# Mixer A of a two-mixer transformer block: the low part of a pair's queries four projection blocks later

## Chip, cores and metric

One core of a Trainium2 chip (trn2) runs the kernel as one program. The metric is the device time of one execution in microseconds (us). PE is TensorE, DVE VectorE, ACT ScalarE, POOL GpSimd and SP SyncE, which issues the DMAs.

## The reference, cut to what matters

The input runs through two blocks of layers. The first block has a mixer A (grouped attention with a rotary encoding over rows and columns) and a mixer B (neighbourhood attention), each on 512 tokens of `x` and 256 tokens of context. The change lies in mixer A:

```python
def gqa_axial_mixer(hx, hc, w_in, q_g, k_g, w_out, cos, sin, need_ctx_out):
    px = hx @ w_in
    q = px[..., :A_WIDTH].reshape(b, t, A_HEADS, HEAD_DIM)        # 16 heads of 64
    ...
    z = px[..., A_WIDTH + 2 * A_KV_WIDTH:]                        # the gate
    q = apply_axial_rope(rms_norm(q, q_g), cos, sin)
    ...
        s = jnp.einsum('bqkgd,bskd->bkgqs', qi, k_all).astype(jnp.float32) * ATTN_SCALE
        p = jax.nn.softmax(s, axis=-1).astype(v_all.dtype)
        return jnp.einsum('bkgqs,bskd->bqkgd', p, v_all)
    ...
    yx = (o * jax.nn.silu(z)) @ w_out
    ...
    qc = rms_norm((hc @ w_in[:, :A_WIDTH]).reshape(b, lc, A_HEADS, HEAD_DIM), q_g)
    zc = hc @ w_in[:, A_WIDTH + 2 * A_KV_WIDTH:]
    sc = jnp.einsum('bqkgd,bskd->bkgqs', qc, kc).astype(jnp.float32) * ATTN_SCALE
```

Everything is float32. A matrix product is made of three on PE: each operand is split into a high part (a rounded copy) and a low part (what the rounding left), and high x high, high x low and low x high are summed.

## The kernel before, in words

**Order of the work.** `build` first writes a list, `plan`, of named items with `do(...)` (L331). Then each engine walks the whole list and issues its own instructions for the items that it has a part in (`program`, L1441). So an engine's queue has the order of the list, and semaphores join the engines. PSUM banks are handed out by rings (`Ring.take`, L160), and the first matmul into a bank waits for the bank's last reader.

**Mixer A.** The 16 heads are worked on in 8 pairs. A pair has six score steps (tiles of 128 queries): four tiles of `x`, with 768 keys (weight 1.0 for the planner), and two of the context, with 256 keys (weight 0.7). So steps 6p to 6p+5 belong to pair p, 48 in all. In a step (`scores` L678, `trans` L698, `outp` L708): PE makes the scores of both heads into all four banks of one ring (L1551), DVE takes maxima (L2170, L2179), ACT exponentials (L1830), DVE reciprocals (L2186), POOL multiplies (L2560), PE transposes the probabilities (L1561) of the step before, ACT and DVE copy them out (L1840, L2195), and PE makes the outputs (L1586) of two steps before, which DVE multiplies with the gate (L2206, for the last pair L2208).

**The fill.** Between these, PE works on projections, drawn block by block from the generator `fill_a` (L861). For pair 1 to 7 it holds four groups of 8 blocks: the queries of `x` and of the context (`query_group`), and the gate of `x` (`gate_group(pair, 0, ...)`) and of the context (`gate_group(pair, 1, ...)`). A block is one of eight slices of the inner dimension, three matmuls, over 512 columns for `x` (5.12 units) or 256 for the context (2.56 units) (`pj` L411; PE L1463 to L1465). `fill_in` (L715) gives each half of a step its share of the units that are left, and stops early at a negative value (`PAUSE`). The dictionary `between` names what is emitted after a block: `between.get(k)` is called when the generator is resumed after block k, ahead of block k+1. After the fill of pair 7 comes `begin_out` (L828), the first blocks of the output projection: per block of `k` a part 0 to 6 (`parts`: ACT cast L1792, then a subtraction on POOL, L2534, for even `k`, on DVE, L2090, for odd), then two blocks of 5.12.

**The query's chain.** While a pair's gate is projected, its queries are finished: sums and turn on PE (L1528, L1534), rotation on DVE and POOL (L2134, L2553, L2140), `a_query_high` (ACT cast, L1812), `a_query_low` (DVE subtraction, L2144: `qL = qT - qH`). The scores read `qH` and `qL`. `query_low(pair)` (L782) plans `a_query_low` and adds the pair to `ready_q`. Tile 0 of a pair isn't planned before (L809 to L811), and `attention` (L665) draws more blocks until it is:

```python
while not todo[n][0]():
    x = more()
```

`a_gate` (ACT L1820, DVE L2150) ends each gate group. In pair 7 the context's gate group carries a modulation unit as well: `ride_mm_x` after block 3 (16 matmuls, L1476, into bank 6) and `ride_tr` after block 6 (L1484).

Of the kernel before, what the change touches and what calls it, by code (L numbers as in the profile page):

```python
# [166 lines left out]
def build(nc, wu, vp, cc, cs1, xt, biasb, pos, out):  # L167
    ctx = ExitStack()
    with ctx:
# [92 lines left out]
        def bank(b, n=512):  # L262
            return PS[:, 512 * b:512 * b + n]
# [67 lines left out]
        def do(*item):  # L331
            plan.append(item)
            done_work[0] += COST.get(item[0], 0)
# [9 lines left out]
        def ring(*groups):  # L343
            return Ring(Order, *groups)
# [66 lines left out]
        def pj(key, un, lo, hi, f0, phase, o, ks=range(8)):  # L411

            groups[key] = Group(key, un.n, False, lo, hi, f0, 128, phase, o)
            for k in ks:
                if k % 4 == 3:
                    tick()
                do("proj", key, k)
                yield (hi - lo) / 100
# [238 lines left out]
        def until(cond):  # L657
            while not cond():
                yield BLOCK
# [89 lines left out]
        OA, FA, FX, FC = ring((5,)), ring((6,), (7,)), ring((6,)), ring((7,))  # L749
# [7 lines left out]
        def query_group(pair, j, pr, between={}):  # L757

            if j == 0:
                aun[pair] = Unit("aqz", pair)  # L760
            lo, hi = FULL[j]
            o = bank(pr.take(("aq", pair, j), (s_qraw, (pair, j))))
            for k in range(8):
                yield from pj(("aq", pair, j), aun[pair], lo, hi, 0, "a", o, (k,))
                between.get(k, nothing)()
            do("a_query_raw", pair, j)

        def query_sums(pair, pr):
            aqps[pair, "sums"] = bank(pr.take(("aqs", pair), (s_qvar, (pair,))))
            do("a_query_sums", pair)  # L770

        def query_turn(pair, pr):
            aqps[pair, "rot"] = bank(pr.take(("aqr", pair), (s_qsin, (pair,))))
            do("a_query_turn", pair)

        def query_rope(pair):
            do("a_query_rope", pair)

        def query_high(pair):
            do("a_query_high", pair)  # L780

        def query_low(pair):  # L782
            do("a_query_low", pair)
            ready_q.add(pair)

        def gate_group(pair, j, pr, between={}):
            lo, hi = FULL[j]
            o = bank(pr.take(("az", pair, j), (s_gate, ("a", pair, j))))
            for k in range(8):
                yield from pj(("az", pair, j), aun[pair], lo, hi, 128, "a", o, (k,))  # L790
                between.get(k, nothing)()
            do("a_gate", pair, j)
            if j:
                ready_z.add(pair)
                aun[pair].done(s_proj, "az", pair, 1)
# [32 lines left out]
        def begin_out(name, phase, part, done, pr):  # L828


            un = Unit(name, 0)
            led = {(m, 0): bank(pr.take((name, m, 0), (s_res, (name, m, 0)))) for m in (0, 1)}
            for k in range(10):
                if k < 7:
                    yield from until(lambda: k in done)
                    part(k)
                    yield 3 if k not in (1, 2) else PAUSE
                if k >= 3:
                    for m in (0, 1):
                        yield from pj((name, m, 0), un, 0, T, 128 * m, phase, led[m, 0], (k - 3,))  # L840
            begun[name] = un, led
# [19 lines left out]
        def fill_a():  # L861
            for pair in range(1, 8):
                yield from query_group(pair, 0, FX, {2: ride_mm, 6: ride_tr})
                yield PAUSE
                yield from query_group(pair, 1, FC)
                yield PAUSE
                yield from until(lambda: pair < 2 or 6 * pair - 7 in scored_a)
                yield from gate_group(pair, 0, FX, {2: lambda: query_sums(pair, FC), 3: lambda: query_turn(pair, FC), 5: lambda: query_rope(pair), 7: lambda: query_high(pair)})
                yield PAUSE
                yield from gate_group(pair, 1, FC, {1: lambda: query_low(pair), **({3: ride_mm_x, 6: ride_tr} if pair == 7 else {})})  # L870
                yield PAUSE
            yield from begin_out("aout", "o", parts_a, done_a, FA)
        values((0, 1))
# [15 lines left out]
        query_high(0)  # L889
        run(gate_group(0, 1, vr, {3: lambda: query_low(0)}))  # L890
        attention("a", [s for pair in range(8) for s in steps_a(pair)], SA, TA, PbA, PTbA, OA, fill_a(), (8 * 14 * (T + LC) + 14 * T) / 100 + 5 * 3, posted_a, scored_a.add)
        do("a_last_gate")

# [459 lines left out]
        OC, FC = ring((4,)), ring((5,), (6,), (7,))  # L1353
# [1495 lines left out]
```

## Time and profile before

| | before |
|---|---|
| median of 3 runs | 1624.19 us (1623.81 to 1627.51) |
| the profiled execution | 1623.98 us |
| its span | 1622.2 us |
| mean granted TensorE clock | 0.978 |
| PE busy | 1534.7 us (95%) |
| DVE busy | 754.4 us (47%) |
| ACT busy | 640.9 us (40%) |
| POOL busy | 688.1 us (42%) |

Times of a row are counted from the start of the span. Mixer A's score steps run from 110 to about 458 us. Matmuls overlap: the duration of a group is from the start of its first to the modelled end of its last, and the next one may start before that. A granted clock of 1.00 is 2.4 GHz, 0.50 is 1.2 GHz.

### The profile page before, as it was taken

The numbers are of one execution on the slowest core, as the hardware profiler recorded it, in microseconds if no ns is written. First come the engines' busy times: TensorE is split into PE (matmuls) and PEld (weight loads), VectorE is DVE, ScalarE is ACT, GpSimd is POOL, SyncE is SP. The second block draws the span as 40 slices with busy tenths as digits, with TensorE's granted clock in tenths as the row PEclk, the third lists the DMA queues.
The fourth block names the chain that finished last, engine by engine and source line by source line (L and its number), as shares of the span: only waits on it lengthen the run. The fifth ranks groups of instructions, "written<-read, shape, count | busy, mean of one in ns | idle before, by whom it ended". The sixth has DMA issues, their size and how long they took to land.

```text
span 1622.2 us, 25653 instructions
## 1 busy us (share of the span) xinstructions
PE 1534.7 (95%) x10114; PEld 1244.3 (77%) x10114; DVE 754.4 (47%) x1733; ACT 640.9 (40%) x1339; POOL 688.1 (42%) x660
## 2 busy tenths in 40 slices
PE   5999999999899999999998899999999989999997
PEld 3887777777688788787876687878787867766875
DVE  4444555555532534534355454733432564455253
ACT  4234444444532533433334353434332344443331
POOL 2534444443432533433325444535255434444462
PEclk8999999999999999999999999999999999999998
DMA  9111111110233222322321222222131221111221
GB/s 396 44 67 38 42 53 53 53 53 28 72 100 128 78 72 82 108 79 79 105 92 43 100 85 78 79 68 88 52 104 53 92 91 53 53 53 53 94 88 52
DMA packets 22438, 129.80 MB, mean 80 GB/s; under 512 B 2480, under 2 KB 2608, under 8 KB 8368
## 3 DMA queue, kind: packets, MB, share of 16 engines
q1 hardware_dynamic: 22176, 127.92, 22.8%
q8 instruction: 80, 1.31, 0.3%
q10 hardware_dynamic: 144, 0.26, 0.1%
q14 instruction: 38, 0.31, 0.1%
HBM read 126.08 MB, written 2.10 MB: 79 GB/s over the span
## 4 chain that ended last, share of the span: by engine, by line
PE 80%; DVE 9%; ACT 3%; POOL 3%; issue 3%; DMA 1%; SPq 0%; POOLq 0%; DVEq 0%; ACTq 0%
PE PS L1463 15%; PE PS L1465 15%; PE PS L1464 15%; PE PS L1586 6%; PE PS L1561 6%; PE PS L1544 4%; PE PS L1458 3%; PE PS L1459 3%; PE PS L1460 3%; PE PS L1551 3%; DVE sm L2170 2%; PE PS L1639 1%; PE PS L1631 1%; PE PS L1476 1%; DMA XC<-in_xt 1%
## 5 line engine op out<-in xcount | busy, mean ns | idle before, releaser
L2493 POOL TENSOR_TENSOR WL<-W,WH 128x512 fp32r<-128x512 f32 x304 | 400.4, 1332 | 330.9 <-ACT WH L1742 330.6
L1463 PE MATMUL PS<-HX,WH 128*128 128x512 f32 x1008 | 420.3, 417 | 11.8 <-DVE LX L2083 3.9
L1465 PE MATMUL PS<-HX,WL 128*128 128x512 f32 x1008 | 399.1, 396 | 0.0
L1464 PE MATMUL PS<-LX,WH 128*128 128x512 f32 x1008 | 398.2, 395 | 0.0
L1463 PEld LDWEIGHTS PS<-HX,WH 128*128 128x128 f32 x1008 | 193.1, 192 | 62.0 <-issue 17.1
L1465 PEld LDWEIGHTS PS<-HX,WL 128*128 128x128 f32 x1008 | 192.0, 190 | 42.6
L1464 PEld LDWEIGHTS PS<-LX,WH 128*128 128x128 f32 x1008 | 192.7, 191 | 35.8 <-issue 2.6
L1742 ACT CAST WH<-W 128x512 fp32r<-128x512 f32 x320 | 186.8, 618 | 42.0 <-PE PS L1460 25.6
L1830 ACT ACTIVATE AR<-PS,sm 128x768 f32<-128x768 f32 (+4 forms) x160 | 115.7, 723 | 165.2 <-DVE sm L2175 93.7
L2170 DVE TENSOR_REDUCE sm<-PS 128x1 f32<-128x512 f32 (+4 forms) x224 | 149.9, 669 | 43.7 <-PE PS L1551 39.3
L2560 POOL TENSOR_SCALAR AR<-AR,sm 128x768 f32<-128x768 f32 (+1 forms) x96 | 77.1, 804 | 186.2 <-DVE sm L2186 186.0
L2560 POOL TENSOR_SCALAR XC<-XC,sm 128x512 f32<-128x512 f32 x64 | 45.1, 704 | 163.2 <-DVE sm L2186 163.2
L1561 PE MATMUL PS<-C,AR 128*128 128x128 f32 x608 | 101.9, 285 | 10.0 <-DVE AR L2206 9.9
L1840 ACT COPY AR<-PS 128x512 f32<-128x512 f32 (+1 forms) x112 | 62.2, 556 | 109.4 <-PE PS L1561 108.4
L1586 PE MATMUL PS<-AR 128*64 128x128 f32 x1408 | 96.7, 282 | 5.8 <-DVE AR L2195 4.1
L1830 ACT ACTIVATE XC<-PS,sm 128x512 f32<-128x512 f32 x64 | 44.2, 690 | 145.2 <-DVE sm L2175 145.2
L1561 PEld LDWEIGHTS PS<-C,AR 128*128 128x128 f32 x608 | 69.3, 142 | 35.8 <-DVE AR L2206 12.8
L1458 PE MATMUL PS<-WH,HX 128*128 128x256 f32 x320 | 95.0, 297 | 0.8 <-POOL WL L2493 0.8
L1463 PE MATMUL PS<-HC,WH 128*128 128x256 f32 (+1 forms) x304 | 95.1, 313 | 0.5 <-POOL LC L2517 0.5
L1586 PEld LDWEIGHTS PS<-AR 128*64 128x64 f32 x1408 | 77.1, 139 | 23.9 <-issue 11.6
L1459 PE MATMUL PS<-WH,LX 128*128 128x256 f32 x320 | 91.2, 285 | 0.0
L1460 PE MATMUL PS<-WL,HX 128*128 128x256 f32 x320 | 91.2, 285 | 0.0
(290 smaller groups left out, 2546.3 us busy)
## 6 DMA issues: line engine op xcount, KB each, us to landing
W<-in_wu SPq DMA_DIRECT2D x98, 1024.0 KB, 4.9
AR<-in_wu SPq DMA_DIRECT2D x8, 1024.0 KB, 11.1
AR<-in_biasb SPq DMA_DIRECT2D x32, 256.0 KB, 2.7
XX<-in_xt SPq DMA_DIRECT2D x2, 1024.0 KB, 6.2
out<-XX SPq DMA_DIRECT2D x8, 256.0 KB, 2.2
XX<-in_xt SPq DMA_DIRECT2D x2, 768.0 KB, 5.3
XC<-in_xt SPq DMA_DIRECT2D x1, 1024.0 KB, 14.2
C<-in_cc SPq DMA_DIRECT2D x1, 770.5 KB, 8.7
```

The lines of the kernel that those rows point to most:

```text
L1458: e.matmul(o, xh, wh, start=(k == 0), stop=False)
L1459: e.matmul(o, xl, wh, start=False, stop=False)
L1460: t = e.matmul(o, xh, wl, start=False, stop=(k == 7))
L1463: e.matmul(o, wh, xh, start=(k == 0), stop=False)
L1464: e.matmul(o, wh, xl, start=False, stop=False)
L1465: t = e.matmul(o, wl, xh, start=False, stop=(k == 7))
L1561: t = e.transpose(o[:, j * 128:j * 128 + 128], s.pb[h][:, (q0 + j) * 128:(q0 + j) * 128 + 128], c("id"))
L1586: t = e.matmul(s.out[h], s.values[h][j], s.pt[h][:, j * 128:j * 128 + 128], start=(j == 0 and s.first), stop=(j == nv - 1 and s.final))
L1742: e.copy(WH[:, PART[n], a:z], W[:, n % 2, a:z]).then_inc(*s_wh.by(n, q))
L1830: e.activation(s.pb[h][:, 0:s.n], PS[:, s.score[h]:s.score[h] + s.n], ACT.Exp, bias=smn[:, i % 4:i % 4 + 1], scale=(1.0 if s.scale is None ...
L2170: e.tensor_reduce(mx, x, AX.X, ALU.max).then_inc(*s_max.by(name, n, h))
L2493: e.tensor_tensor(WL[:, d, a:z], W[:, n % 2, a:z], WH[:, d, a:z].bitcast(F32), ALU.subtract).then_inc(*s_wl_pool.by(n, q))
```

## The change

In the context's gate group `query_low(pair)` is called after block 5 and not after block 1, for pairs 1 to 7. Pair 0 has a call of its own, which stays. Nothing else is edited; the planner derives the rest of the list from it.

```diff
@@ -867,7 +867,7 @@
                 yield from until(lambda: pair < 2 or 6 * pair - 7 in scored_a)
                 yield from gate_group(pair, 0, FX, {2: lambda: query_sums(pair, FC), 3: lambda: query_turn(pair, FC), 5: lambda: query_rope(pair), 7: lambda: query_high(pair)})
                 yield PAUSE
-                yield from gate_group(pair, 1, FC, {1: lambda: query_low(pair), **({3: ride_mm_x, 6: ride_tr} if pair == 7 else {})})
+                yield from gate_group(pair, 1, FC, {5: lambda: query_low(pair), **({3: ride_mm_x, 6: ride_tr} if pair == 7 else {})})
                 yield PAUSE
             yield from begin_out("aout", "o", parts_a, done_a, FA)
```

## Rows read from the trace of the kernel before

**Rows 1.** The page: PE's busy time, and the chain that ended last.
```profile
PE 1534.7 (95%) x10114; PEld 1244.3 (77%) x10114; DVE 754.4 (47%) x1733; ACT 640.9 (40%) x1339; POOL 688.1 (42%) x660
...
PE 80%; DVE 9%; ACT 3%; POOL 3%; issue 3%; DMA 1%; SPq 0%; POOLq 0%; DVEq 0%; ACTq 0%
```

**Rows 2.** Waits of PE, 100 to 470 us: us in total, times, longest.
```profile
PE PS L1551 <- ACT AR L1830: 3.0, 3, 1.9
PE PS L1551 <- DVE XX_parts L2144: 2.1, 1, 2.1
```

**Rows 3.** The source line L2144: duration ns min/median/max, first and last start us.
```profile
L2144 DVE TENSOR_TENSOR XX_parts<-AR,XX_parts x8: 939/940/1202, 108.2 to 412.7; 128x768 fp32r<-128x768 f32 x8
```

**Rows 4.** Timeline, pair 2, steps 11 and 12: start us, us, engine line [idle before].
```profile
154.11 0.15 DVE L2186 RECIPROCAL sm<-sm 128x1 f32<-128x1 f32 x1
...
155.38 1.32 PE L1551 MATMUL PS<-AR_parts,XX_parts 64*128 64x512 f32 x12
```

**Rows 5.** Timeline, pair 5: the last reciprocal of step 29, and score 30.
```profile
328.82 0.16 DVE L2186 RECIPROCAL sm<-sm 128x1 f32<-128x1 f32 x1 [0.66 <-ACT AR L1830]
328.99 1.33 PE L1551 MATMUL PS<-AR_parts,XX_parts 64*128 64x512 f32 x12
```

**Rows 6.** Timeline, pair 6: last reciprocal of step 35, scores 36 and 37.
```profile
369.42 0.16 DVE L2186 RECIPROCAL sm<-sm 128x1 f32<-128x1 f32 x1
...
369.82 1.32 PE L1551 MATMUL PS<-AR_parts,XX_parts 64*128 64x512 f32 x12
...
375.29 1.32 PE L1551 MATMUL PS<-AR_parts,XX_parts 64*128 64x512 f32 x12 [0.82 <-ACT AR L1830]
```

**Rows 7.** Timeline, pair 7: context blocks 1 and 2, gate product, a_query_low, score 42.
```profile
410.75 0.28 PE L1463 MATMUL PS<-HC,WH 128*128 128x256 f32 x1
...
411.11 0.28 PE L1463 MATMUL PS<-HC,WH 128*128 128x256 f32 x1
...
412.05 0.69 DVE L2150 SCALAR_TENSOR_TENSOR AR<-AR,PS 128x512 f32<-128x512 f32 x1 [1.40 <-ACT AR L1820]
412.65 0.95 DVE L2144 TENSOR_TENSOR XX_parts<-AR,XX_parts 128x768 fp32r<-128x768 f32 x1
...
413.75 1.32 PE L1551 MATMUL PS<-AR_parts,XX_parts 64*128 64x512 f32 x12 [2.12 <-DVE XX_parts L2144]
```

**Rows 8.** Timeline, step 42 after its score: modulation, second exponential's end, score 43, its maximum.
```profile
416.31 1.07 PE L1476 MATMUL PS<-W,sm 128*32 128x256 f32 x16
...
418.86 0.18 ACT L1830 ACTIVATION_READ_ACCUMULATOR AR<-PS,sm 128x1 f32 x1
...
420.36 1.33 PE L1551 MATMUL PS<-AR_parts,XX_parts 64*128 64x512 f32 x12
...
421.71 0.96 DVE L2170 TENSOR_REDUCE sm<-PS 128x1 f32<-128x768 f32 x1 [0.41 <-PE PS L1551]
```

**Rows 9.** Timeline: score 44, subtractions of part 1, outputs in steps 44 and 45.
```profile
426.45 1.73 PE L1551 MATMUL PS<-AR_parts,XX_parts 64*128 64x512 f32 x12 [1.88 <-ACT AR L1830]
...
427.68 1.05 DVE L2090 TENSOR_TENSOR LX<-AR,HX 128x512 fp32r<-128x512 f32 x1 [2.42 <-ACT HX L1792]
...
428.65 0.94 DVE L2090 TENSOR_TENSOR LC<-AR,HC 128x256 fp32r<-128x256 f32 x1
...
429.98 2.83 PE L1586 MATMUL PS<-AR 128*64 128x128 f32 x24 [1.80 <-DVE AR L2195]
...
438.85 1.53 PE L1586 MATMUL PS<-AR 128*64 128x128 f32 x24
```

**Rows 10.** Stretches of 2 us: busy us of engines, PEclk (granted clock), DMA share, GB/s.
```profile
427.00:429.00 2.00, 1.18 (x10) 0.82 (x6) 1.32 (x2) 2.00 (x6) 2.00 (x2) 0.54 0.00 0
429.00:431.00 2.00, 1.02 (x10) 1.02 (x12) 1.97 (x5) 0.26 (x1) 1.22 (x3) 0.50 0.03 8
431.00:433.00 2.00, 2.00 (x19) 1.67 (x16) 0.25 (x2) 0.00 (x0) 1.93 (x3) 0.50 0.00 0
433.00:435.00 2.00, 2.00 (x11) 1.82 (x11) 0.92 (x3) 1.10 (x2) 0.00 (x0) 0.76 0.00 0
```

## The prediction

> **What bounds the kernel now.** I read the page first. TensorE (PE) is busy for 95% of the span and holds 80% of the chain of work that ended last [rows 1]: an engine other than PE costs time only where PE stands and waits for it. Then I asked who waited for whom on PE in mixer A (100 to 470 us). The operation that the change moves, a_query_low on VectorE (DVE, L2144), ends a PE wait once in the whole kernel, for 2.1 us; the exponentials on ScalarE (ACT, L1830) end three waits of 3.0 us in total [rows 2]. The eight a_query_low take 0.94 us each, one of them 1.20 [rows 3]. So the change works on what is behind 0.94 us of DVE work, and it can only matter where PE has little in hand.
>
> For the places I need the order of the program. Its planner writes one list, and every engine runs its own part of it in that order. A score step n takes all four banks of the score ring, so its matmuls wait for both exponentials of step n-1; the first step of a pair (6 x pair) also waits for that pair's a_query_low, and it isn't planned before `ready_q` holds the pair. I worked through the planner from the units that it spends: a context block costs 2.56, an x block 5.12, and a step's half draws blocks until its share is spent. What follows "four blocks later" differs by pair. Note that a function between two blocks is emitted when the generator is resumed, that is ahead of the next block.
>
> **Pairs 1 to 4: same blocks, later DVE slot, 0 us.** Block 5 is the last one drawn in the first score step of the group, so a_query_low slips into the following step, behind that step's first reciprocal and ahead of the gate product, still before the first score step of the pair. For pair 2 that reciprocal starts at 154.11 and takes 0.15, so the operation would run from about 154.2 to 155.1; score 12 starts at 155.38 [rows 4]. It stays hidden by some 0.2 us, by the two context blocks and the chain of exponentials. The old slot cost PE nothing either, so nothing is won. Bounds: 0 (hidden) and 0.1 us each if it takes its longest duration [rows 3]; I take 0.
>
> **Pair 5: +0.95 us.** Here the group began half a step later, and the operation lands behind the second reciprocal of step 29, one step-half before score 30. That reciprocal starts at 328.82 and takes 0.16; score 30 starts at 328.99, right behind PE's last block [rows 5]. After the change DVE does 0.94 us between the two: 329.9, and with the 0.05 of a semaphore score 30 starts at about 329.95. Nothing covers it, since the remaining blocks are before it already. Below: 0, if the reciprocal comes earlier because a_query_low no longer stands ahead of step 29's maxima; but the second of these waits in DVE's order behind the output of step 27, which that does not move.
>
> **Pair 6: +0.65 us.** Block 5 is the last one drawn before score 36, so the planner has to draw block 6 as well to emit a_query_low. PE does the same work (0.36 us for a context block, from one block's start to the next one's [rows 7]), but score 36 is now behind it and behind DVE: the reciprocal at 369.42, then 0.94, so 370.45 where it was 369.82 [rows 6]. And this delay is not absorbed: score 37 stood waiting for ACT for 0.82 us [rows 6], so the chain from score 36 sets its time, and the block moved ahead is no cover there. Bounds 0.35 (the block alone) and 0.9 (the operation at its longest).
>
> In one row more (the 1.20 us instance) a_query_low ran beside a probability product of GpSimd (POOL) that had just started, the other seven had 0.94 to 0.97. The Trainium skill, GPSIMD Engine Reference, section 1, says that GpSimd's SBUF interfaces are shared with VectorE and contend with DVE instructions that have two SBUF inputs, which this one has; by it 0.26 us would come on top in pairs 5 and 6, so +2.1 in place of +1.6.
>
> **Pair 7: -1.4 us.** Here the real change of order is. The step before it is through with the x group when score 42 is due, and the planner is forced on until a_query_low is out. Before: context blocks 0 to 2, then score 42, which stood idle for 2.12 us until a_query_low had ended at 413.60 [rows 7]. After: blocks 0 to 6, with the modulation unit that rides after block 3 (16 matmuls, 1.0 us [rows 8]), then score 42. DVE's order doesn't change (gate product of the x group, then a_query_low), as the blocks put nothing on DVE. PE reaches the modulation unit at 412.0; it needs bank 6, which that gate product frees at 412.75 (412.05 + 0.69 [rows 7]). So 412.8 + 1.0 + three blocks of 0.36 = 414.9 for score 42, 1.15 us later than before. From a score step's start to the end of its second exponential was 5.29 us (413.75 to 418.86 + 0.18), and score 43 came at 420.36, because the modulation's small matmuls and block 7 stood ahead of it [rows 8]. These are out of the way now: score 43 at 414.9 + 5.3 + 0.1 = 420.3, unchanged. The idle 2.12 us has become some 0.8 ahead of score 42 and some 2.2 ahead of score 43.
>
> Then the planner's parts of the output projection (ACT cast, then a DVE or POOL subtraction) come a step earlier: parts 0 and 1 in step 42 rather than 43. The two DVE subtractions of part 1 (1.05 and 0.94 us [rows 9]) then stand ahead of the maximum of score 43 and wait for the casts, which end about 422.6: I get the maximum at 424.1 rather than 421.71 [rows 8]. Score 44 moves from 426.45 [rows 9] to some 428.4, with two blocks of the output projection (0.7 us each, an estimate from twice the context block) already done before it. Part 3 does the same to the maximum of score 44, once more about 2.2 us; but there the kernel before had its own stall of that size, for parts 1 and 2 stood at that place (429.98, PE idle 1.80 [rows 9]). So I find score 45 at its old time, 437.5, with two more blocks done, and steps 46 and 47, which PE bounds, are 2 x 0.7 = 1.4 us shorter. Bounds of the whole term: -3.3 (with the clock, below) and +2.4 (one of the two delays of a maximum, 424.1 less 421.7, is not absorbed and eats the gain).
>
> **The DMAs.** SP's queue is moved in one thing: the weight load that waits for the riding modulation unit goes out with it, 3.5 us sooner, and the reload of x behind it as well. Neither is waited for here. No instruction is added or taken out.
>
> **The clock.** PE is granted 2.4 GHz (1.00) up to 427 us, and then 0.54, 0.50, 0.50 and 0.76 over four stretches of 2 us, so half (1.2 GHz) until 434 [rows 10], behind a stretch with its idle waits ahead of scores 42 to 44. By rows it costs 2.83 - 1.53 = 1.3 us on one step's output matmuls [rows 9], and I add half of that for the six transposes behind them, which ran in it too: 1.9, an estimate. I assume that it falls once after the change as well, as the idle sum of this stretch is nearly the same. The Trainium skill, TensorE: Matmul & The Clock Gate, in its Terms, prices throttled time at that time x (1 - K/N), so 6.9 us x 0.5 = 3.4 us here; by it the fall that stays away would be worth -3.4, not -1.9. It says (Part 1) that recent activity is what releases the throttle: that speaks against the change where it takes cover away from behind score 42.
>
> **Sum.** 0 + 0.95 + 0.65 - 1.4 = +0.2 us. The profiled execution took 1623.98 us (a span of 1622.2 and 1.8 around it), so 1624.2 by its own time. The median of the runs is 1624.19, 0.2 above it, so 1624.4. About 0.3% (4.9 us) is what a measurement of this kernel can tell from no change.
>
> **The rivals.**
> B: the operation stays hidden everywhere and the planner's shift in pair 7 evens out; 1624.2. For it: PE's wait on a_query_low is 2.1 of 1622 us. Against it: rows 5 and 6 leave no room. Chance 0.15.
> C: the clock does not fall in step 44, since its idle time is spread differently, and pair 7 gives 1.4 + 1.9: 1624.4 - 1.9 = 1622.5, and 1620.9 if pairs 5 and 6 cost nothing too. For it: two blocks now lie ahead of score 44, where PE stood. Against: idle time after block 7 is new. Chance 0.20.
> D, slower: the subtractions of parts 1 and 3 in DVE's queue ahead of the maxima of scores 43 and 44 both reach the end, because the cover went before score 42. Each is 2.4 us, the 1.4 is gone: 1.6 + 4.8 = +6.4, so 1630.6. It decides if score 45 comes more than some 3 us later than 437.6. Against: PE had idle time there of the same size already. Chance 0.10.
> My forecast, near zero by cancelling terms: 0.55.
>
> The forecast's own range goes from -3.3 (1620.9) to 1.6 + 0.5 + 2.4 = +4.5 (1628.7); it takes in B and C, and leaves out D and the tails. Over 4.9 us faster needs nearly all idle time of steps 42 to 44 to vanish: 0.03. Slower by as much is most of D: 0.09. The same: 0.88.
>
> **What would show it.** Pairs 1 to 4: distances between the first scores of the pairs unchanged. Score 30 behind a_query_low with some 0.9 us of PE wait that is new, score 36 likewise with less. The 2.1 us wait ahead of score 42 gone or under 1 us, a new wait for ACT of 2 us ahead of score 43, and score 43 at 422 (420.4 and the 1.6 of pairs 5 and 6). The end of step 47 within 2 us of the old one. I am wrong if the pairs 1 to 4 shift, if the blocks are drawn elsewhere than I worked out, if the clock falls at another place or twice, or if anything behind 460 us changes its length.

## The result, and the profile after

| | before | after |
|---|---|---|
| median, runs side by side on one chip | 1624.72 us (10 runs, 1622.61 to 1627.51) | 1629.93 us (10 runs, 1627.55 to 1633.42) |
| the profiled execution | 1623.98 us | 1627.55 us |
| its span | 1622.2 us | 1625.6 us |
| mean granted TensorE clock | 0.978 | 0.977 |

The changed kernel is slower: the ratio is 1.0029, 95% interval 1.0019 to 1.0038, about 4.7 us. The forecast was +0.2 us with a range that ended at 1628.7. The median of 1629.93 lies 1.2 us beyond that. The difference is clear of the noise, though still inside the 0.3% that the prediction took as its bound.

The page of the kernel after, first two parts of it that answer to [rows 1]:

```profile
PE 1536.0 (94%) x10114; PEld 1245.5 (77%) x10114; DVE 755.9 (47%) x1733; ACT 640.8 (39%) x1339; POOL 689.1 (42%) x660
...
PE 78%; DVE 9%; ACT 4%; POOL 3%; issue 3%; DMA 1%; SPq 0%; POOLq 0%; DVEq 0%; ACTq 0%
```

No instruction was added (the same counts), and PE's share of the chain fell from 80 to 78%: the loss is waiting. The waits of PE, 100 to 470 us (us in total, times, longest), which answer to [rows 2]:

```profile
PE PS L1561 <- DVE AR L2206: 11.3, 13, 2.8
PE PS L1551 <- ACT AR L1830: 3.3, 3, 2.2
PE PS L1586 <- ACT AR L1840: 2.8, 3, 1.2
...
PE PS L1551 <- DVE XX_parts L2144: 1.1, 2, 0.9
PE PS L1561 <- DVE AR L2208: 1.1, 2, 0.8
PE PS L1476 <- DVE AR L2150: 0.8, 1, 0.8
```

The 2.1 us wait on a_query_low is gone. Two smaller ones on it have come (0.9 and 0.2), and one of 0.8 ahead of the modulation unit. Two groups of waits have grown or come that the prediction doesn't name: the outputs (L1586) for ACT's copies (2.8 us, before 0.9) and the transposes (L1561) for L2208 (1.1 us, before none).

**Pairs 5 and 6.** Timeline after, answering to [rows 5, 6] (start us, us, engine line):

```profile
326.84 0.16 DVE L2186 RECIPROCAL sm<-sm 128x1 f32<-128x1 f32 x1 [0.65 <-ACT AR L1830]
326.92 0.94 DVE L2144 TENSOR_TENSOR XX_parts<-AR,XX_parts 128x768 fp32r<-128x768 f32 x1
327.10 1.10 POOL L2560 TENSOR_SCALAR AR<-AR,sm 128x256 f32<-128x256 f32 x1 [0.34 <-DVE sm L2186]
...
328.00 1.32 PE L1551 MATMUL PS<-AR_parts,XX_parts 64*128 64x512 f32 x12 [0.93 <-DVE XX_parts L2144]
...
368.39 0.94 DVE L2144 TENSOR_TENSOR XX_parts<-AR,XX_parts 128x768 fp32r<-128x768 f32 x1
...
369.48 1.32 PE L1551 MATMUL PS<-AR_parts,XX_parts 64*128 64x512 f32 x12 [0.21 <-DVE XX_parts L2144]
```

The two profiled executions can be laid on each other instruction by instruction. Up to score 30 the one after is 1.98 us ahead; 1.6 of that comes from a half-clock stretch that only before has, at 147 us, and is no work of the change. Behind score 30 it is 0.99 ahead, behind score 36 0.34: so +0.99 and +0.65. In both places a_query_low took 0.94 us although POOL worked beside it; what got longer was POOL's product (1.10 us at 327.10, where the one of the same size just before took 0.48).

**Pair 7.** Timeline after, steps 42 to 44, answering to [rows 7, 8, 9]:

```profile
411.64 0.69 DVE L2150 SCALAR_TENSOR_TENSOR AR<-AR,PS 128x512 f32<-128x512 f32 x1 [1.40 <-ACT AR L1820]
...
412.38 1.07 PE L1476 MATMUL PS<-W,sm 128*32 128x256 f32 x16 [0.80 <-DVE AR L2150]
...
414.64 1.32 PE L1551 MATMUL PS<-AR_parts,XX_parts 64*128 64x512 f32 x12
...
420.11 2.04 PE L1551 MATMUL PS<-AR_parts,XX_parts 64*128 64x512 f32 x12 [2.17 <-ACT AR L1830]
...
421.88 1.67 DVE L2090 TENSOR_TENSOR LX<-AR,HX 128x512 fp32r<-128x512 f32 x1 [1.11 <-ACT HX L1792]
...
424.35 0.94 DVE L2170 TENSOR_REDUCE sm<-PS 128x1 f32<-128x768 f32 x1
...
429.53 1.82 PE L1551 MATMUL PS<-AR_parts,XX_parts 64*128 64x512 f32 x12
```

Start of each score step, and how long each lasts (from its start to the next one's; the last to the first block of the context's output projection, 458.66 and 459.39):

| step | 42 | 43 | 44 | 45 | 46 | 47 |
|---|---|---|---|---|---|---|
| starts, before | 413.75 | 420.36 | 426.45 | 437.56 | 444.60 | 451.60 |
| starts, after | 414.64 | 420.11 | 429.53 | 437.56 | 445.50 | 452.36 |
| lasts, before | 6.61 | 6.09 | 11.11 | 7.04 | 7.00 | 7.06 |
| lasts, after | 5.47 | 9.42 | 8.03 | 7.94 | 6.86 | 7.03 |

The execution after enters pair 7 with 0.41 ahead (its gate product at 411.64, before at 412.05) and leaves it 0.73 behind: +1.14 us where -1.4 was forecast. Score 42 comes 1.30 late by that measure; steps 42 to 44 then take 22.92 us where they took 23.81, so 0.41 of delay is left at score 45; step 45 adds 0.90; steps 46 and 47 give back 0.17 and not 1.4. What happens in steps 45 to 47, first before, then after:

```profile
437.43 0.69 DVE L2090 TENSOR_TENSOR LX<-AR,HX 128x512 fp32r<-128x512 f32 x1 [1.59 <-ACT HX L1792]
...
438.91 0.96 DVE L2170 TENSOR_REDUCE sm<-PS 128x1 f32<-128x768 f32 x1
...
444.62 0.58 ACT L1840 COPY AR<-PS 128x512 f32<-128x512 f32 x1
...
445.86 1.53 PE L1586 MATMUL PS<-AR 128*64 128x128 f32 x24 [0.64 <-DVE AR L2195]
445.92 1.14 ACT L1742 CAST WH<-W 128x512 fp32r<-128x512 f32 x2
...
456.12 0.66 PE L1586 MATMUL PS<-AR 128*64 128x128 f32 x8 [0.46 <-ACT AR L1840]
```

```profile
438.73 1.26 DVE L2090 TENSOR_TENSOR LX<-AR,HX 128x512 fp32r<-128x512 f32 x1 [1.66 <-ACT HX L1792]
...
440.25 0.94 DVE L2170 TENSOR_REDUCE sm<-PS 128x1 f32<-128x768 f32 x1
...
441.69 0.44 PE L1561 MATMUL PS<-C,AR 128*128 128x128 f32 x2 [0.77 <-DVE AR L2208]
...
445.54 1.14 ACT L1742 CAST WH<-W 128x512 fp32r<-128x512 f32 x2
...
446.58 0.58 ACT L1840 COPY AR<-PS 128x512 f32<-128x512 f32 x1
...
447.30 1.53 PE L1586 MATMUL PS<-AR 128*64 128x128 f32 x24 [1.18 <-ACT AR L1840]
...
456.86 0.66 PE L1586 MATMUL PS<-AR 128*64 128x128 f32 x8 [1.13 <-ACT AR L1840]
```

In step 45 the subtraction of part 5 stands ahead of the maximum, at 440.25 instead of 438.91; L2208 is behind that maximum in DVE's queue, and PE waits 0.77 for it. In steps 46 and 47 PE has one block less each (0.79 us from start to start), and its waits ahead of the outputs grow from 0.64 to 1.18 and from 0.46 to 1.13. The two steps lose their gain in different ways.

- Step 46: the wait stands ahead of the missing block, so the block's absence can't have made it. From the outputs to score 47 the step is 0.68 us shorter (451.60 - 445.86 before, 452.36 - 447.30 after). From score 46 to the outputs it is 0.54 longer (1.26 before, 1.80 after), because ACT now has the two weight casts (L1742, drawn together with the blocks) ahead of the copy that the outputs wait for: that copy starts at 446.58, where before it started at 444.62 and the casts came behind it at 445.92.
- Step 47: the missing block lay between its score and the wait at 456.86, and that distance is the same as before (4.50 and 4.52 us). It is set by the chain of maximum, exponential and ACT's copy, so here the saved work has become waiting.

**Mixer A in sum:** 0.99 + 0.65 - 0.07 (won back between score 36 and pair 7) + 1.14 = +2.7 us. The comparison says 4.7, so 2 us are left for what lies behind mixer A; in these two profiled executions it is 2.6. Where no granted clock differs the two executions keep their distance to some 0.03 us for hundreds of microseconds; it jumps only where one has half-clock time that the other hasn't. Stretches (PE, PEld, DVE, ACT, POOL busy us, then granted clock, DMA share, GB/s) of before, then of after:

```profile
840.00:1000.00 160.00, 144.08 (x775) 115.20 (x775) 86.88 (x149) 72.55 (x135) 76.97 (x68) 0.95 0.25 83
1000.00:1200.00 200.00, 200.00 (x1041) 167.04 (x1040) 85.80 (x136) 76.03 (x134) 85.95 (x73) 0.97 0.22 72
1200.00:1500.00 300.00, 291.12 (x1750) 219.55 (x1749) 147.14 (x418) 117.06 (x284) 139.53 (x145) 1.00 0.20 67
```

```profile
840.00:1000.00 160.00, 144.85 (x779) 116.52 (x776) 86.78 (x148) 71.95 (x134) 76.85 (x68) 0.93 0.24 82
1000.00:1200.00 200.00, 200.00 (x1045) 166.65 (x1044) 86.59 (x137) 76.53 (x135) 85.37 (x73) 0.98 0.22 74
1200.00:1500.00 300.00, 291.23 (x1743) 219.68 (x1743) 147.10 (x418) 117.04 (x284) 139.83 (x146) 0.99 0.20 67
```

After loses 1.9 us in 840 to 1000, 1.5 around 1305 and 0.8 around 1610, and gets 1.6 back around 1030, where only before ran at half clock.

### The profile page after: what moved, and what is told of

Its sections match the earlier page's. It is cut to its first block, busy times and chain, and to the rows that moved or that the text cites. A ratio compares the mean times of both kernels' runs of the same rounds, so it can differ in the third digit from the quotient of the medians.

```text
span 1625.6 us, 25653 instructions
## 1 busy us (share of the span) xinstructions
PE 1536.0 (94%) x10114; PEld 1245.5 (77%) x10114; DVE 755.9 (47%) x1733; ACT 640.8 (39%) x1339; POOL 689.1 (42%) x660
## 4 chain that ended last, share of the span: by engine, by line
PE 78%; DVE 9%; ACT 4%; POOL 3%; issue 3%; DMA 1%; SPq 0%; POOLq 0%; DVEq 0%; ACTq 0%
PE PS L1463 15%; PE PS L1465 15%; PE PS L1464 15%; PE PS L1586 6%; PE PS L1561 6%; PE PS L1544 4%; PE PS L1458 3%; PE PS L1459 3%; PE PS L1460 3%; PE PS L1551 2%; DVE sm L2170 2%; PE PS L1639 1%; PE PS L1631 1%; PE PS L1476 1%; POOL WL L2493 1%
## 5 line engine op out<-in xcount | busy, mean ns | idle before, releaser
L1742 ACT CAST WH<-W 128x512 fp32r<-128x512 f32 x320 | 186.7, 618 | 43.1 <-PE PS L1460 25.1
L2560 POOL TENSOR_SCALAR AR<-AR,sm 128x768 f32<-128x768 f32 (+1 forms) x96 | 78.9, 822 | 184.1 <-DVE sm L2186 184.1
L2560 POOL TENSOR_SCALAR XC<-XC,sm 128x512 f32<-128x512 f32 x64 | 44.8, 700 | 164.7 <-DVE sm L2186 164.7
L1561 PE MATMUL PS<-C,AR 128*128 128x128 f32 x608 | 101.3, 283 | 12.6 <-DVE AR L2206 11.3
L1840 ACT COPY AR<-PS 128x512 f32<-128x512 f32 (+1 forms) x112 | 62.2, 555 | 108.0 <-PE PS L1561 107.1
L1586 PE MATMUL PS<-AR 128*64 128x128 f32 x1408 | 95.9, 281 | 5.2 <-ACT AR L1840 3.5
L1561 PEld LDWEIGHTS PS<-C,AR 128*128 128x128 f32 x608 | 68.5, 141 | 38.9 <-DVE AR L2206 14.4
L1586 PEld LDWEIGHTS PS<-AR 128*64 128x64 f32 x1408 | 76.3, 138 | 23.1 <-issue 13.2
```

The lines of the kernel that those rows point to most:

```text
L1561: t = e.transpose(o[:, j * 128:j * 128 + 128], s.pb[h][:, (q0 + j) * 128:(q0 + j) * 128 + 128], c("id"))
L1586: t = e.matmul(s.out[h], s.values[h][j], s.pt[h][:, j * 128:j * 128 + 128], start=(j == 0 and s.first), stop=(j == nv - 1 and s.final))
L1742: e.copy(WH[:, PART[n], a:z], W[:, n % 2, a:z]).then_inc(*s_wh.by(n, q))
```

## The experiments

All are edits of one of the two kernels and were timed side by side with the kernel before in runs taken alternately. "Its mixer A" is how far the profiled execution falls behind the one of before between 100 and 480 us. The half-clock time of a run is 2 x (1 - mean granted clock) x span; before has some 78 us of it.

**The change by pairs.** The new place for some pairs only, the old one for the rest.

```diff
-                yield from gate_group(pair, 1, FC, {1: lambda: query_low(pair), ...
+                yield from gate_group(pair, 1, FC, {5 if pair < 5 else 1: lambda: query_low(pair), ...
```

> Only pairs 1 to 4 have the low part behind block 5. Theory M (the cost is where PE waits for the moved operation, in pairs 5 to 7): nothing, within 0.5 us of before. Rival K (the cost comes from the granted clock, which depends on when each stretch falls): the trace of the changed kernel lacks one half-clock stretch at 147.3 us that the kernel before had, and pair 1's step was 1.6 us shorter for it; by K this kernel shows such a difference of 1 to 2 us in either direction, and further ones behind 470 us.

> Only pairs 5 and 6. Theory M: score 30 waits some 0.95 us for the low part and score 36 comes 0.65 us later, so +1.6 us, and it stays to the end. Rival K: these 1.6 us are there at 470 us, but the end is off by other amounts, with half-clock stretches behind 800 us at other places than before. A third theory (slack later takes it back): 0.

> Only pair 7: four context blocks and the modulation unit ahead of score 42. Theory M from the trace of the changed kernel: score 42 comes 1.3 us later, score 44 some 3 us later, and the end of mixer A 1.2 us later than before: +1.2. My prediction's term was -1.4. Rival K: the part of the cost that the trace of the changed kernel does not show inside mixer A (4.7 us by the ratio of the runs, less 2.8 us by the trace) lies here, as further half-clock time: +3 us.

> The changed kernel again (pairs 1 to 7), for a second trace and as the sum to which the other three should add up: 4.7 us over before (ratio 1.0029). Theory M: the drift against before is +1.0 at score 30, +0.65 more at score 36 and +1.2 more over steps 42 to 47, as in the first trace. Rival K: half-clock stretches stand at other places than in the first trace of the same program, and move the end by some us.

| kernel | median us (runs) | ratio to before, interval | mixer A us |
|---|---|---|---|
| before | 1625.61 (23) | | |
| pairs_1_4 | 1626.26 (12) | 1.0002 [0.9992, 1.0012] | 0 and a half-clock stretch |
| pairs_5_6 | 1632.25 (7) | 1.0034 [1.0020, 1.0048] | +0.93 and +0.61 at scores 30 and 36; +0.9 in step 44 by a longer half-clock stretch, given back by 530 us |
| pair_7 | 1630.34 (7) | 1.0028 [1.0013, 1.0043] | +1.18 over steps 42 to 47 |
| all_late (the changed kernel) | 1630.53 (8) | 1.0028 [1.0014, 1.0042] | +0.99, +0.60, +1.12 |

Pairs 1 to 4 cost nothing. The others cost in mixer A what the trace of the full change shows, 1.54 and 1.18. But their measured times don't add up: by the ratios 5.5 us for pairs 5 and 6 alone, 4.6 for pair 7 alone, 4.6 for all. Each half of the change is 3 to 4 us dearer than its own waits (4.0 and 3.4), the whole only 1.9. Their half-clock time differs the same way, 93, 87 and 81 us on average, where before had 78 in the same set of runs; why the halves get more of it than the whole is not shown. With 7 or 8 runs of each, an interval is some 2.3 us wide to either side. pair_7, with no edit in pairs 5 and 6, has the very waits of steps 45 to 47:

```profile
441.63 0.44 PE L1561 MATMUL PS<-C,AR 128*128 128x128 f32 x2 [0.78 <-DVE AR L2208]
447.25 1.53 PE L1586 MATMUL PS<-AR 128*64 128x128 f32 x24 [1.18 <-ACT AR L1840]
456.80 0.66 PE L1586 MATMUL PS<-AR 128*64 128x128 f32 x8 [1.12 <-ACT AR L1840]
```

**Parts held back.** Pair 7 late, and one more pause, so that the parts of the output projection come in their old step: this undoes the one consequence and keeps the other.

```diff
                 yield PAUSE
+            yield PAUSE
             yield from begin_out("aout", "o", parts_a, done_a, FA)
```

> Pair 7 alone is late, and one more PAUSE ahead of the output projection's first parts puts parts 0 and 1 back behind score 43, where they were before. Theory M (the subtractions of part 1 in VectorE's queue delay the maximum of score 43, and score 44 with it): score 44 comes at its old distance of some 6.1 us behind score 43, not 9.4, and the 1.2 us that pair 7 alone cost at the end of mixer A are gone. Rival (the four blocks taken from behind score 42 are what costs): the 1.2 us stay. For the total, theory K (later stages depend on when they start) says that with the shift the rest goes too: within 1 us of before.

1627.23 us (12 runs) against 1626.23 (29): 1.0008 [0.9997, 1.0020], where pair_7 had 1.0028 [1.0013, 1.0043]: the times point the expected way, but their intervals overlap. The maximum of score 43 comes 2.29 us behind its score's start, and not 4.24:

```profile
420.68 2.29 PE L1552 MATMUL PS<-AR_parts,XX_parts 64*128 64x512 f32 x12 [2.17 <-ACT AR L1831]
422.97 0.96 DVE L2171 TENSOR_REDUCE sm<-PS 128x1 f32<-128x768 f32 x1 [1.64 <-PE PS L1552]
...
428.32 1.31 PE L1552 MATMUL PS<-AR_parts,XX_parts 64*128 64x512 f32 x12 [1.32 <-ACT AR L1831]
```

Score 44 came 7.6 us behind score 43 and not 6.1 as expected; score 43's 12 matmuls ran at half clock and took 2.29 us. So the expected gain at the end of mixer A did not show in this execution: it fell 2.1 us behind before over mixer A, all of it in steps 43 and 44, where it has some 7 us more of half-clock time than before has.

What it does show cleanly is steps 45 to 47. They are as long as before (6.98, 7.04 and 7.07 us; before 7.04, 7.00 and 7.06; the changed kernel 7.94, 6.86 and 7.03), without a wait on L2208, and with the waits of before ahead of the outputs:

```profile
448.15 1.53 PE L1587 MATMUL PS<-AR 128*64 128x128 f32 x24 [0.68 <-DVE AR L2196]
...
458.43 0.66 PE L1587 MATMUL PS<-AR 128*64 128x128 f32 x8 [0.46 <-ACT AR L1841]
```

So the 0.9 us of step 45, and the longer waits of steps 46 and 47, come from parts and blocks being drawn a step earlier.

**A pure delay.** Before, with 5 or 15 overwritten 512-column matmuls (1.15 or 3.45 us) at the start of mixer A's output projection; the changed kernel with 3 (0.7 us); and before with the same 5 in the last projection of the kernel. The first real matmul into the same bank overwrites what they wrote.

```diff
+                    if k == 0 and g == ("aout", 2, 0):
+                        for _ in range(5):
+                            e.matmul(o, wh, xh, start=True, stop=True)
                     e.matmul(o, wh, xh, start=(k == 0), stop=False)
```

> The kernel before with five more matmuls of 512 columns (results overwritten) at the start of group m=2 of the output projection of mixer A, where TensorE is dense: a pure delay of 1.15 us (5 x 0.23). Order and mixer A are untouched. Theory K: later half-clock stretches depend on when a stage starts, so the trace shows +1.15 at 600 us and some 2.5 to 3 behind 930 us, and the runs come out 3 to 5 us over before. Rival P (a delay is a delay): +1.15 throughout, 1.2 us over before.

> The same with fifteen matmuls, 3.45 us. Rival P: +3.45 throughout, three times the other. Theory K: the later stages move by 3.45 us, about the distance between neighbouring half-clock stretches in the traces, so that they fall at their old places in the program: 3.4 us over before and no more, that is hardly more than five matmuls cost, or less.

> The changed kernel with three more matmuls at the same place, 0.7 us more work. Its stages behind mixer A are then 2.7 + 0.7 = 3.4 us later than before. Theory K: the half-clock stretches come back to their old places in the program and the total is 3.4 us over before, less than the changed kernel without the added work (4.8 over). Rival P: 0.7 us over the changed kernel, 5.5 over before.

> The kernel before with the same five overwritten matmuls (1.15 us), but in the last projection of the whole program (group m=2 of the second block's output) and not behind mixer A. Theory K (a delay costs more than itself because it moves the later stages to where they lose more half-clock time): almost nothing comes after it, so the mean granted clock stays that of before (0.976) and the runs come out 1.2 us over before, where the same five matmuls behind mixer A gave 0.9735 and 2.9 us. Rival E (any edit of the program lowers the clock, wherever it is): 0.974 and some 3 us here too.

| kernel | ratio to before, interval | that is | put in | half-clock us |
|---|---|---|---|---|
| before_plus_5 | 1.0018 [1.0008, 1.0029] | +2.9 | 1.15 | 86 |
| before_plus_15 | 1.0019 [1.0010, 1.0028] | +3.1 | 3.45 | 84 |
| late_plus_3 | 1.0041 [1.0028, 1.0054] | +6.7 | 0.7, and the change | 91 |
| before_plus_5_at_end | 1.0010 [1.0001, 1.0019] | +1.6 | 1.15 | 80 |

1.15 us of delay measures as 2.9 and 3.45 us as 3.1. So an excess isn't proper to the change, though the lower end for before_plus_5 is 1.3 us, hardly above the 1.15 that a plain delay would give. In these runs and those of the pairs, what the time holds beyond the traced waits or the added work goes from -0.4 us (before_plus_15) to +4.0 (pairs_5_6). late_plus_3 (five runs) speaks against theory K as it was put: the half-clock stretches should have come back to their old places and the time to 3.4 us over before, and 6.7 came, with the 5.5 of the rival inside the interval. before_plus_5_at_end came out near the 1.2 of theory K, but the interval just reaches the 3 of its rival too. It has nothing in front of its last stage that is changed, and yet its profiled execution, the slowest of its eleven runs, is 4.6 us off by 1320 us: where the later half-clock stretches fall varies from one execution of the same instructions to the next.

**Other orders at that place.** low_7_early plans a_query_low of pair 7 in the group before; part_1_on_pool gives part 1's subtraction to POOL, in the kernel before; the third does both.

```diff
-... 7: lambda: query_high(pair)})
+... 7: lambda: [query_high(pair)] + ([query_low(pair)] if pair == 7 else [])})
```
```diff
-                parts("o", k, j, zT.at(k, lo, hi), after, "pool" if k % 2 == 0 else "dve")
+                parts("o", k, j, zT.at(k, lo, hi), after, "pool" if k % 2 == 0 or k == 1 else "dve")
```

> The other way round: in pair 7 the low part is made right behind the high part, ahead of the x group's gate product on VectorE and of the context's gate group in the plan; pairs 1 to 6 as before. By the rows of before VectorE could start it at 411.6 instead of 412.65, so score 42 comes at 412.65, 1.1 us sooner, and three context blocks (1.1 us) lie behind it as cover. Theory M: score 43 comes 1.5 us sooner and mixer A ends 1 to 2 us sooner. Theory K: any shift of the later stages can cost half-clock time, so the total may be 0 to 3 us over that. Rival: score 42 is not what sets the time of steps 43 and 44, 0.

> The kernel before with the two subtractions of part 1 on GpSimd instead of VectorE. Before, VectorE did them from 427.7 to 429.6, and the copy that the outputs of step 42 wait for came behind them at 429.5, with TensorE idle for 1.8 us. Theory M (VectorE's queue is what delays steps 43 to 45): TensorE resumes some 1.3 us sooner and mixer A ends 1 to 1.5 us sooner. Rival: GpSimd then holds up the products of step 43 and the clock falls anyway, 0.

> Both of these edits. Theory M: 2 to 3 us sooner than before at the end of mixer A. Theory K: what of it arrives at the end depends on the half-clock time of the later stages, between 0 and 3 us faster than before.

low_7_early: 1627.44 us (12 runs) against 1624.93 (29), 1.0015 [1.0004, 1.0026], a miss. In the profiled execution, the slowest of the twelve, score 42 came 1.0 us sooner by the distance to before, but behind its own wait of 2.18 us the clock fell, and score 43 lost more than that:

```profile
415.65 2.04 PE L1551 MATMUL PS<-AR_parts,XX_parts 64*128 64x512 f32 x12 [2.18 <-DVE XX_parts L2144]
...
424.08 1.32 PE L1551 MATMUL PS<-AR_parts,XX_parts 64*128 64x512 f32 x12
```

The granted clock there:

```profile
412.00:416.00 4.00, 1.82 (x10) 1.23 (x11) 2.43 (x3) 2.22 (x4) 2.62 (x3) 1.00 0.14 16
416.00:420.00 4.00, 4.00 (x29) 3.35 (x26) 2.07 (x6) 1.07 (x2) 0.00 (x0) 0.58 0.63 250
```

part_1_on_pool: 1625.73 (11 runs), 1.0002 [0.9993, 1.0010]. Its profiled execution gains 2.7 us in mixer A, where 1 to 1.5 was expected and where it also has less half-clock time than before, and gives 1.9 back behind it; its runs have 84 us of half-clock time. Both together: 1627.35 (12), 1.0007 [0.9993, 1.0020]. The profiled execution of this one is the fastest of its twelve (1619.86). It has the same wait of 2.18 us ahead of score 42, but the clock stayed full there, score 43 kept 0.7 us of the 1.0 that score 42 had won, and mixer A ended 2.3 us sooner: so the fall in low_7_early's trace is not bound to that order of the work.

**Is it the clock of the later stages?** Overwritten matmuls (two instructions and some 0.85 us each), one or two in each of seven of PE's long waits between the stages (1.6 to 2.7 us), in before, in the changed kernel, and in before with the five matmuls.

```diff
+            def warm(o, n):
+                for _ in range(n):
+                    e.matmul(o, c("ones"), C[:, 0:512], start=True, stop=True)
...
+                    warm(G.out, {("bq", 0): 2, ("bout", 0, 0): 2}.get(g, 0))
...
+                 warm(N.sums[p], {"c": 2, "e": 2}.get(name, 0))
...
+                    warm(rbout[name][:, 0:512], {"b": 1, "d": 2, "e": 1}.get(name, 0))
```

> The kernel before, with one or two overwritten 512-column matmuls (some 0.85 us each in the traces) in each of seven of TensorE's longest waits between the stages (2.32, 2.17, 1.61, 2.70, 1.67, 2.59 and 2.56 us in the trace of before). Theory H (the part of the change's cost that lies behind mixer A is half-clock time of the later stages): the mean granted clock rises above before's 0.976 and the runs lie closer together; the time is 0 to 4 us less if the matmuls stay inside the waits, at 0.26 us for each us of half clock that goes. Rival I (the rest is something other than the clock): nothing is said of this kernel but the fillers' own length where they stick out, 0 to +3 us.

> The changed kernel with the same fillers; to be read against warm_before. Theory H: the difference to warm_before shrinks from 4.7 us to the 2.7 to 2.8 us that the trace shows inside mixer A, since the later stages have the same clock in both. Rival I: the difference stays at 4.7 us or so. If the fillers don't raise the clock, the run decides nothing.

> warm_before with the five overwritten matmuls of before_plus_5 (1.15 us) at the start of mixer A's output projection; to be read against warm_before. Theory H: +1.15 us. Rival I: about +3 us, as before_plus_5 measured against before. If the fillers don't raise the clock, the run decides nothing.

| kernel | median us (runs) | ratio to before, interval | half-clock us |
|---|---|---|---|
| before | 1626.07 (29) | | 77 |
| warm_before | 1625.42 (11) | 0.9995 [0.9987, 1.0004] | 63 |
| warm_late | 1627.97 (12) | 1.0012 [1.0001, 1.0022] | 62 |
| warm_plus_5 | 1623.47 (12) | 0.9986 [0.9978, 0.9995] | 63 |

The fillers raise the clock, and in the same stretch as above (840 to 1000 us) it is now alike in warm_before and warm_late:

```profile
840.00:1000.00 160.00, 147.53 (x786) 115.64 (x786) 86.21 (x148) 72.60 (x135) 76.68 (x68) 0.97 0.24 82
```

```profile
840.00:1000.00 160.00, 147.52 (x794) 115.95 (x791) 86.80 (x147) 72.06 (x135) 76.72 (x68) 0.97 0.25 83
```

The change now costs 2.55 us by the medians (1627.97 - 1625.42), as theory H wants (2.7). But by the means it is 2.7 +- 2.0 (twice the standard error), which reaches up to the 4.7 of the rival. And warm_plus_5 is 1.95 us faster than warm_before (1.2 +- 1.5 by the means), where theory H expected 1.15 more and the rival 3 more, though its trace shows the 1.13 us of added work between 440 and 480. Both missed. And warm_before gained 0.65 us by the medians, where 14 us less of half-clock time, at the 0.26 that its expectation took for each, would have been 3.6. So these runs don't settle the theory: the total moves by some 2 us either way, and one agreement within that isn't proof.

**The candidate.** warm_before with part 1's subtraction on POOL.

> warm_before with part 1's subtraction on GpSimd as well, the candidate for a version that beats both kernels. part_1_on_pool lost in later half-clock stretches what it gained in mixer A. Theory H: with the stages' waits filled the gain of 1.6 to 2.7 us reaches the end, so 1623 to 1624, 0.9985 of before. Rival: where the later half-clock stretches fall moves the total by some 2 us either way whatever is gained in front of them, as warm_plus_5 showed (1.95 us less than warm_before with 1.15 us more work): then anything from 1622 to 1627.

1620.84 us (12 runs) against 1626.37 (17): 0.9969 [0.9958, 0.9981], half-clock time 59 us. It beats both kernels, by some 5 us the one before. That is outside both what theory H (1623 to 1624) and what its rival (1622 to 1627) expected: more than the 1.6 to 2.7 us came. How much of that is the gain in mixer A and how much is luck of the clock stays open.

## Why the prediction was wrong, step by step

- **Pairs 1 to 4: 0.** Right; pairs_1_4 measured 1.0002.
- **Pair 5: +0.95, pair 6: +0.65.** Right: +0.99 and +0.65 (0.58 by the start of pair 7), PE waits 0.93 and 0.21 for a_query_low in those places. The sentence that score 37 wouldn't absorb it is right too: it still waits 0.82 for ACT. The 0.26 us that POOL beside it might have added did not come: a_query_low took 0.94 both times.
- **Pair 7, order of the list.** Right: context blocks 0 to 6 and the modulation unit stand ahead of score 42. Score 42 +1.3 against 1.15; a wait of 0.80 for the gate product and 2.17 ahead of score 43, both as worked out; score 43 +0.15 against 0. Its maximum came at 424.35, which is 424.8 with the 0.41 by which this execution entered the pair ahead, against 424.1.
- **Score 44 "from 426.45 to some 428.4".** It came at 429.53, or 429.9 with the same 0.41. The forecast was 0.4 short by its own rows: in before score 44 starts 4.74 us behind the maximum of score 43 (426.45 - 421.71), and 424.1 + 4.74 is 428.8. The later maximum and the clock are the rest. In before the clock was full up to 427; after, two stretches at half clock stand here, one ahead of score 44. The forecast let it fall once and named a second fall as what would make it wrong:

```profile
420.00:422.00 2.00, 1.89 (x12) 1.68 (x12) 0.62 (x3) 2.00 (x6) 1.13 (x2) 0.61 0.03 9
422.00:424.00 2.00, 2.00 (x14) 1.43 (x12) 2.00 (x2) 0.15 (x1) 2.00 (x2) 0.54 0.00 0
...
427.00:429.00 2.00, 2.00 (x8) 1.56 (x6) 1.21 (x5) 1.15 (x3) 0.91 (x1) 0.56 0.00 0
429.00:431.00 2.00, 2.00 (x12) 1.25 (x12) 0.35 (x2) 2.00 (x5) 1.48 (x2) 0.58 0.00 0
431.00:433.00 2.00, 2.00 (x32) 1.70 (x31) 2.00 (x3) 0.05 (x1) 2.00 (x2) 1.00 0.03 8
```

  Both fell behind a PE that had stood still (2.17 us at 418 to 420, 1.68 ahead of 425.8), and it was full again at 431 where before it was half until 434 [rows 10]; so the sum is about the same, and "I find score 45 at its old time" came out nearly right (+0.4). Rival D, by its own test (score 45 over 3 us late), did not happen, although the measured 1629.93 lies near its 1630.6.
- **The step that failed:** "with two more blocks done, and steps 46 and 47, which PE bounds, are 2 x 0.7 = 1.4 us shorter". The two blocks were done (2 in step 43, and 3 and 1 in steps 46 and 47 where before had 4 and 2), but PE alone doesn't bound these steps, and 0.17 us is left of 1.4. The rows of before show that other engines set a part of them: PE waits 0.64 for L2195 at 445.86 and 0.46 for L1840 at 456.12. Step 47 hangs on its exponentials and ACT's copy from its score to that second wait (4.52 us before, 4.50 after), so its block bought 0.03. Step 46 did get 0.68 shorter behind its outputs, and lost 0.54 of it ahead of them, because the weight casts had moved up in ACT's queue as well, ahead of the copy. With the parts held back (p7_parts_held) these waits are 0.68 and 0.46 again; no run moves the casts alone.
- **A term left out:** the parts move up by a step in every step, not only parts 1 and 3. Part 5's subtraction then stands ahead of the maximum of score 45: +0.9. These two, 1.2 and 0.9, and the 0.4 at score 45 are the 2.5 us between -1.4 and +1.14.
- **Behind mixer A: nothing.** Wrong by some 2 us (2.6 in the profiled executions), which I put at zero without pricing it. By the trace it is half-clock time in later stages. It isn't settled that a later start of those stages causes more of it as a rule: before_plus_5 (+1.8 beyond its work) and warm_plus_5 (-3.1) point opposite ways. Which executions at which shift get the extra stretches stays open.

The likely sign of the change was in reach: with 0.95 + 0.65 sure and pair 7's return resting on a cover that was not read, the chance of a small slowdown should have been the largest, and the range should have had at least 2 us more on either side for the clock.

## What to carry to other kernels

Work moved forward out of a later step shortens that step only where its engine is the bound: look up that engine's waits in the step itself, and whether they stand ahead of the missing work or behind it, before counting the saving. A planner that feeds every queue moves the other engines' work too, in each later step, and an in-order queue puts it ahead of something. A kernel with many short stalls has a clock term of a few microseconds that depends on where they fall; a difference of 0.2% is direct cost only as far as a trace shows the waits, and an experiment that shifts the rest without work of its own says how large that term is.

## What the runs showed of the hardware that was not expected

- **The clock's share of the time.** Over the 318 runs of all these kernels that have a clock on record the span goes with the half-clock time at 0.26 +- 0.02 us for each us of it, with a level of its own for each kernel and 1.2 us of scatter left (here and below, +- is twice the standard error). The Trainium skill, TensorE: Matmul & The Clock Gate, in its Terms, prices it at (1 - K/N), so 0.5; these runs show half of that. It differs by place: where only one of the two profiled executions of before and after has half-clock time, a us of it moved them apart by 0.47 us around 1030, 0.43 around 1305 and 0.28 in 840 to 1000. That would fit if PE waits for others in a part of its half-clock time; it was not tried by itself. At equal half-clock time the changed kernel is 3.0 +- 0.6 us slower than before, which is the 2.7 of its trace; pair_7 2.1 +- 1.0, pairs_5_6 1.9 +- 1.0, p7_parts_held -0.1 +- 0.8, before_plus_5 0.6 +- 0.8, part_1_on_pool -1.7 +- 0.8. The fillers don't fit this line (warm_before +3.5 at equal half-clock time): that suits half-clock time taken away where PE only waited, which is worth nothing, but it is argued, not shown.
- **The same program at different clocks.** low_7_early_part_1_on_pool had mean granted clocks between 0.969 and 0.979 in its twelve runs, and times from 1619.86 to 1631.22 us.
- **DVE subtractions beside POOL's.** L2090 over 128x512 took 1.67 and 1.26 us where POOL worked beside it (L2534, and L2560 behind it), and 0.69 at 437.43 and 444.44 in before, where POOL stood idle. The Trainium skill, GPSIMD Engine Reference, section 1, has these two contend for SBUF; this trace agrees, and in pair 5 it was POOL's operation that got longer (1.10 us where 0.48 was usual), not DVE's. In pair 7 the contention lengthened the very operations that stood ahead of the maxima of scores 43 and 45, by 1.0 and 0.6 us.
